# One more use of an adding DMA: the weights' low parts in the memory and attention phases of a hybrid encoder

## The reference

```python
for i in range(DEPTH):                                   # 2 layers
    h = rmsnorm(x, pre_g[i]); mem_n = rmsnorm(mem, mem_g[i])
    # layer 0: Mamba-2 SSD mixer; layer 1: neighbourhood attention, 32 heads
    proj = h @ w_in                                      # z, mixer inputs, q_mem
    kv = (mem_n @ w_mem_kv)                              # keys and values of 256 memory tokens
    m = softmax(q_mem k^T / 16) v                        # 4 memory heads of 256
    mixed = concat([mixer(proj), m]) * silu(z)           # (layer 0 norms the mixer part)
    x = x + rmsnorm(mixed @ w_out[i], post_g[i])
```

## Time and profile before

| | |
|---|---|
| time, median of 3 runs | 2127.89 us (2126.92 to 2128.80) |
| profiled execution, its own time | 2128.9 us |
| its span | 2127.1 us |
| TensorE busy | 2083.0 us (98%) |
| TensorE weight loads (beside the matmuls) | 1774.5 us (83%) |
| VectorE / ScalarE / GpSimd busy | 1074.4 / 799.7 / 883.1 us |
| bytes moved by DMA | 211.96 MB, mean 100 GB/s |
| adding DMAs, issued by GpSimd | 53, of 512 KB each |
| stores of `macc_dram` and `x1_dram` | 3072 KB each |
| a load of decay rows (`acs_dram`, line 1291), 16 times | 1536 KB each |
| residual and partial-sum loads in layer 1's memory phase | 512 KB each |
| residual loads at the end (line 2145) | 1536 and 1024 KB |

### The profile page before, as it was taken

How to read it: one execution, slowest core, us unless ns; L and a number is a source line. 1 busy time by engine, 2 the same in 40 slices (tenths; PEclk the granted TensorE clock), 3 DMA queues, 4 the chain that set the end, 5 groups by cost and what they waited for, 6 DMA issues and landing times.

```text
span 2127.1 us, 30983 instructions
## 1 busy us (share of the span) xinstructions
PE 2083.0 (98%) x12412; PEld 1774.5 (83%) x12412; DVE 1074.4 (51%) x1880; ACT 799.7 (38%) x1943; POOL 883.1 (42%) x676
## 2 busy tenths in 40 slices
PE   8999999999999999999999999999999999999997
PEld 7888887788888888877888887888888888888885
DVE  4104332598898889887602223154333414542446
ACT  4123122465564656653322211143324323432353
POOL 5533332232333332225733332664454445544543
PEclk9999999999999999999999999999999999999998
DMA  5221112466666566566421111322131223122213
GB/s 188 90 71 53 51 50 77 151 153 150 149 154 150 146 154 164 139 163 195 159 68 50 51 50 57 113 65 69 52 96 59 59 61 95 57 60 81 67 51 119
DMA packets 214316, 211.96 MB, mean 100 GB/s; under 512 B 24764, under 2 KB 173532, under 8 KB 214173
## 3 DMA queue, kind: packets, MB, share of 16 engines
q1 hardware_dynamic: 206541, 182.20, 28.3%
q0 software_dynamic: 7632, 27.79, 6.9%
HBM read 168.19 MB, written 12.21 MB: 85 GB/s over the span
## 4 chain that ended last, share of the span: by engine, by line
PE 51%; DVE 3%; issue 1%; ACT 0%; DMA 0%; POOL 0%; DVEq 0%; POOLq 0%
PE bank L246 25%; PE bank L301 9%; PE bank L647 6%; PE bank L2485 2%; PE bank L2513 2%; PE bank L1140 2%; PE bank L2496 2%; PE bank L1166 1%; DVE acc L1013 1%; PE bank L1204 1%; DVE acc L1017 1%; PE bank L520 0%; DVE acc L1007 0%; DMA R<-macc_dram 0%; PE bank L2557 0%
## 5 line engine op out<-in xcount | busy, mean ns | idle before, releaser
L246 PE MATMUL bank<-Hh,Wh 128*128 128x512 f32 (+1 forms) x1936 | 652.8, 343 | 4.8 <-ACT R L1342 1.5
L246 PE MATMUL bank<-Hl,Wh 128*128 128x512 f32 (+1 forms) x1936 | 640.6, 337 | 0.0
L246 PE MATMUL bank<-Hh,Wl 128*128 128x512 f32 (+1 forms) x1936 | 566.4, 336 | 1.2 <-DMA Wl<-Wraw 1.1
L190 POOL TENSOR_SCALAR Wh<-Wraw 128x1024 fp32r<-128x1024 f32 x164 | 176.3, 1075 | 742.2 <-issue 555.9
L246 PEld LDWEIGHTS bank<-Hh,Wh 128*128 128x128 f32 x1936 | 367.0, 190 | 52.9 <-issue 12.7
L193 POOL TENSOR_TENSOR Wl<-Wraw,Wh 128x1024 fp32r<-128x1024 f32 x164 | 404.8, 2468 | 13.7
L246 PEld LDWEIGHTS bank<-Hl,Wh 128*128 128x128 f32 x1936 | 367.3, 190 | 37.0 <-issue 1.7
L246 PEld LDWEIGHTS bank<-Hh,Wl 128*128 128x128 f32 x1936 | 348.3, 190 | 40.0 <-DMA Wl<-Wraw 1.6
L371 DVE TENSOR_TENSOR acc<-bank,acc 128x512 f32<-128x512 f32 x240 | 164.0, 690 | 163.3 <-PE bank L301 150.4
L216 POOL TENSOR_SCALAR Wl<-Wraw 128x1024 fp32r<-128x1024 f32 x53 | 68.4, 1291 | 371.8 <-DMA Wraw<-in_ssd_w_in_dram 107.9
L301 PE MATMUL bank<-Wh,Mh 128*128 128x512 f32 x384 | 151.8, 395 | 6.4 <-DVE acc L371 6.4
(11 more groups left out here) (269 smaller groups left out, 3495.2 us busy)
## 6 DMA issues: line engine op xcount, KB each, us to landing
Wraw<-in_na_w_in_dram SPq DMA_DIRECT2D x80, 512.0 KB, 3.7
Wraw<-in_ssd_w_in_dram SPq DMA_DIRECT2D x57, 512.0 KB, 4.0
Wl<-Wraw POOLq DMA_DIRECT2D x53, 512.0 KB, 4.8
Wraw<-in_w_out_dram SPq DMA_DIRECT2D x48, 512.0 KB, 3.3
R<-acs_dram SPq DMA_DIRECT2D x16, 1536.0 KB, 7.5
Wraw<-in_w_mem_kv_dram SPq DMA_DIRECT2D x32, 512.0 KB, 3.9
R<-gs_dram SPq DMA_DIRECT2D x32, 128.0 KB, 3.5
R<-R SPq DMA_DIRECT2D x32, 128.0 KB, 3.4
```

The costliest lines, as they stand in the source:

```text
L190: pool.tensor_scalar(Wh[:, s, :], Wraw[:, s, :], 1.0, 1.0, ALU.mult, ALU.mult).then_inc(pool_c, 1)
L246: mm = pe.matmul(DB[h.k % 2][:, 0:t1 - t0], w[:, k, :], x[:, k, t0:t1], start=(i == 0), stop=(i == 3 * KC - 1))
```

## The change

All units from the third on are made by the adding transfer, in every phase: `split_unit` hands over to `split_unit_by_dma` when `low_count` is positive. Units 0 and 1 (the first two key units, which are multiplied together) stay as they were. In `pe_dense` and `pe_out_tiles` the order with low products last was there already and now applies everywhere. The two loops that have their own code get the same order: in `ValueBlock.tensor` and in the value units of `memory_phase`, all tiles do their four high products first, then, behind one `wait_low`, all tiles do the two low ones. In `out_by_tile` the wait is put ahead of the tile; in `keys_by_group` it does nothing, as units 0 and 1 are not counted.

```diff
         def split_unit(pool):
             u, c = U["pool"], CH["pool"]
+            if low_count(u.k):
+                split_unit_by_dma(pool)
+                return
             s = u.k % 2
...
-        BY_DMA = {}
+        FIRST_BY_DMA = 2
 
         def low_count(unit):
-            first, last = BY_DMA["units"]
-            return unit - first + 1 if first <= unit < last else 0
+            return max(0, unit - FIRST_BY_DMA + 1)
...
                         for k in range(2):
-                            for p, (x, y) in enumerate(((Hh, wh), (Hl, wh), (Hh, wl))):
-                                mm = pe.matmul(self.banks[t][:, :], x[:, 2 * j + k, tok], y[:, k, :],
-                                               start=(j == 0 and k == 0 and p == 0), stop=(j == 3 and k == 1 and p == 2))
+                            for p, x in enumerate((Hh, Hl)):
+                                pe.matmul(self.banks[t][:, :], x[:, 2 * j + k, tok], wh[:, k, :],
+                                          start=(j == 0 and k == 0 and p == 0), stop=False)
+                    wait_low(pe, u.k)
+                    for t in range(NT):
+                        tok = slice(self.tokens[t], self.tokens[t] + P)
+                        for k in range(2):
+                            mm = pe.matmul(self.banks[t][:, :], Hh[:, 2 * j + k, tok], wl[:, k, :],
+                                           start=False, stop=(j == 3 and k == 1))
                         if t == NT - 1:
                             mm.then_inc(unit_done, 1)
                         elif j == 3:
...
                             if g == 0:
                                 pe.wait_ge(w_ready, w.value + u + 3)
+                                wait_low(pe, w.k + u)
...
                         for k in range(2):
-                            for p, (x, y) in enumerate(((Mem_h, wh), (Mem_l, wh), (Mem_h, wl))):
-                                mm = pe.matmul(V_BANK[t][:, :], x[:, 2 * j + k, tok], y[:, k, :],
-                                               start=(j == 0 and k == 0 and p == 0), stop=(j == 3 and k == 1 and p == 2))
+                            for p, x in enumerate((Mem_h, Mem_l)):
+                                pe.matmul(V_BANK[t][:, :], x[:, 2 * j + k, tok], wh[:, k, :],
+                                          start=(j == 0 and k == 0 and p == 0), stop=False)
+                    wait_low(pe, w.k)
+                    for i, t in enumerate(V_ORDER[half]):
+                        tok = slice(t * P, (t + 1) * P)
+                        for k in range(2):
+                            mm = pe.matmul(V_BANK[t][:, :], Mem_h[:, 2 * j + k, tok], wl[:, k, :],
+                                           start=False, stop=(j == 3 and k == 1))
...
             unit0, half0, mix0 = pre.units - 4, pre.half - 8, MX["pe"].k + 4
-            BY_DMA["units"] = pre.units, pre.units + unit_index(PAIRS) - 4 + 2
...
                         pe.wait_ge(w_ready, u.value + (3 if at < 2 else 4))
+                        wait_low(pe, u.k + (0 if at < 2 else 1))
```

## The result

Four runs of the changed kernel gave a median of 2187.66 us (2183.62 to 2192.79), four of the kernel before beside them 2128.35 us (2126.92 to 2130.43). The ratio is 1.0278 (95% interval 1.0262 to 1.0294): 59.3 us slower. I had predicted 2152.5 us, 2135 to 2166. The sign was right, the size less than half of what came.

What follows compares the result with a forecast made beforehand. TensorE, busy 2083.0 of 2127.1 us, was taken to bound the kernel. Terms 4 + 9 + 7 + 0.7 (attention's first key unit) + 5.5 - 1.5 = +24.7 us gave 2153.6, stated as 2152.5 us, range 2135 to 2166.

Steps and rivals of the forecast that it cites:

- What bounds: Whole kernel: TensorE is busy 2083.0 of 2127.1 us; what counts is whether GpSimd's work per unit fits TensorE's unit time.
- Term 1: First layer, value units: GpSimd's period of 6.2 us against 5.7 us per unit on TensorE, +4 us (+1 to +6.5).
- Units of 768 columns or six output tiles (8 us and more on TensorE) leave it hidden: Longer units, including most of attention: they cover the chain negate, add, land, negate, so attention costs and gains nothing there.
- Term 2: Second layer, key units: quiet chain +2.4 us, more from adds behind other loads and sync's queue; +9 us (+2.4 to +13).
- Term 3: Second layer, last two value units: an add lands late behind the `x1_dram` store and the clock falls; +7 us (+4 to +9).
- Term 4: The end, last output unit: whole landing counts, residual loads in flight, clock falls; +5.5 us (+2.4 to +7.5).
- Term 6: Order of the products: the same matmuls, so nothing; perhaps 0.3 us at the change of half, inside other stalls.
- term 5: Gain: GpSimd computes less per unit, shortening TensorE's wait for VectorE shortly before 2076 us; -1.5 us (-3.8 to 0).
- E: Rival, worse: second layer's keys saturate DMA, late residuals hold up VectorE and the turning; beyond +35, near 2170 us; chance 0.15.
- A: Rival: landing about 4.0 us in quiet stages keeps the chain hidden, only the end costs; 2128 to 2131 us; chance 0.06.
- B: Rival: faster through VectorE, its wait before 2076 us and waits for plain splits gone; 2121.8 us; chance 0.04.
- C: Rival: slower at quiet prices, the chain binds but transfers hardly meet; +9.8 us, near 2138 us; chance 0.22.

Runs made afterwards that it cites:

- experiment 5: Changed kernel with one landing semaphore for each slot of `Wl`, so GpSimd's next negation need not wait for the last add: 2173.31 us (1.0211).
- experiment 7: Changed kernel, but the transfer copies `Wraw` over `Wl` instead of adding it (low parts wrong): 2149.04 us (1.0095).
- experiment 4: Kernel before in its splits (only the mixer's units by adding transfer), but with the value units' changed loops, low products last: 2130.04 us (1.0003).
- experiment 6: Changed kernel, but the two loads of `ssd_d` read contiguous rows of 16 numbers instead of single 4-byte pieces: 2173.14 us (1.0204).
- Experiment 8: Changed kernel, but twelve loads of partial sums and residual in the second layer's memory phase move 32 of 1024 columns: 2173.14 us (1.0205).
- experiment 9: Changed kernel with both 32-column loads of partial sums and residual and one landing semaphore for each slot of `Wl`: 2171.09 us (1.0188).
- `attn_plain`: Changed kernel, but the 76 units of the attention phase are split by GpSimd alone: 2178.62 us (1.0235).

## Why the prediction was right in sign and too small

**What bounds** was right: only TensorE's idle time counts, and the loss is where units last 5.6 to 5.7 us on TensorE. The chain negate, add, land, negate became the bound there (experiments 5 and 7), attention hides it (window 1430 to 2110), and the order costs nothing (experiment 4).

**Term 1 was mis-sized, 8 us against 4.** I took the period from one pair of negations in the mixer, 6.2 us. It is 6.39 us over the eight links beside the value units. The unit time was too long as well: my 45.6 us end with a wait of 0.69 us for ScalarE, and a value unit takes TensorE 5.6 us (67.31 to 106.50, seven units). Eight links of 6.39 - 5.6 = 0.8 us make 6.3 us, of 6.7 measured; 1.3 us more had been lost in the key units (the delay goes from 0.6 to 1.9 us before the first value unit), whose loss I had not counted in this layer. One pair of rows was too thin, since with a period so near to the unit time 0.3 us in their difference raise the loss by more than half; my upper bound was +6.5.

**The step that failed outright: "Units of 768 columns or six output tiles (8 us and more on TensorE) leave it hidden".** It compares the quiet period with the unit and never asks which transfers stand ahead of an add at each place. In the first layer's heads these are the small constants of the mixer. In the kernel before they were harmless, since TensorE never waited there (no wait in its rows from 113 to 175 us). An add lands 21.2 us after its issue, and 8 us of cover do not help. It cost +14 us (experiment 6), and the trace of before had the two loads; its line 1308 (now 1323) alone, issued at 119.7 and 120.5:

```profile
DMA to landing us min/median/max: 12.6/17.2/21.8
```

It even had what they do to a transfer behind them. The weight load of 512 KB that sync issued next, and its landing (line 169 alone):

```profile
125.37 0.40 SPq L169 DMA_DIRECT2D Wraw<-in_ssd_w_in_dram  x1
```
```profile
DMA to landing us min/median/max: 18.6/18.6/18.6
```

The four weight loads before it took 3.7 to 4.1 us. I had walked sync's queue for the stages that I costed, not for those that I had called covered.

**Term 2 was mis-sized, 21.0 us against 9 (bound 13).** I started the chain at the second key unit ("the first negation can start at 974.73"). The first one, whose split came 11 us earlier in before, is the worst: its add meets five loads at once. By my own rate, 5.5 us for 1536 KB, 2560 KB would have made 9 us; 5.9 us over quiet were measured. Against 4.7 us quiet, the seven landings (10.6, 9.1, 7.1, 5.1, 5.7, 6.1, 6.2) hold 17.0 us of contention, and two stretched negations 1.8 us; I had counted four or five of 1.8 us. Together with quiet links (7 x 6.45 = 45.2) that is 64.0 us for the measured 63.3. Experiment 8 confirms the split: 13 us go with the loads. I had named sync as a second path for 1.5 us. With the chain's wait gone the key units still lose 12.1 us (experiment 5), and with thin loads 5.6 us (experiment 9), and in both traces every weight load there is issued just after an add has landed. How much sync's wait costs by itself, with the chain in place, was not measured: no run takes that wait away.

**Terms 3, 4 and 6 were right, term 5 in part by luck.** The add beside the `x1_dram` store landed after 10.0 us (11.3 at its twin), TensorE waited 4.0 us for it, and the place lost 7.9 us (+7). The end lost 6.7 us (+5.5), 2.6 of them clock. At VectorE's wait 2.0 us are won (-1.5): the wait fell from 2.1 to 1.6 us, and the clock no longer dropped behind it. The change's own part is the 0.5 us. The wait is 1.3 to 1.7 us in all eleven traces with attention's low parts by transfer and 2.1 to 2.2 us in the three without (before, experiment 4, `attn_plain`); but `attn_plain`, with a wait of 2.19 us, shows a clock of 1.00 behind it. So the 1.5 us of clock can come back without the change, and that the shorter wait is what brought them here is not shown. Attention's first units lost 1.4 us (+0.7), a small term that came out double.

**The rivals.** E, "worse", came closest in time (2170 against 2187.7), and its mechanism is that of the key units (that late residual tiles hold up VectorE was not tested). A and B failed as argued: the add is never under 4.5 us. C's transfers that "hardly meet" failed at the key units. Missing among them was a transfer held up by something other than bytes.

## What to carry to other kernels

When work moves from an engine to a DMA, list for every stage, the covered ones too, what stands in the DMA queues in the microseconds before each new transfer: its landing there is the price, not its quiet duration. A buffer hand-over that waits for a landing puts the whole landing into the period of its units, so convert only units whose time on the bounding engine is well above that period; 34 of 162 converted units made all the loss here, and one of them, with 8 us of cover, more than any other. A result that many units use with slack and a few without it should be priced on the few, each at its own place.

## What the runs showed of the hardware that I had not expected

- A transfer within SBUF that adds takes 4.5 to 4.7 us for 512 KB, the same one as a copy 2.9 us (experiment 7): accumulating costs 1.6 us or more.
- Two loads of 1024 pieces of 4 bytes, 8 KB in all, took up to 21.8 us and delayed a 512 KB transfer from another queue to 21.2 us (19.7 as a copy), while for most of that time the DMA engines' share was 0.05 and no bytes moved. As contiguous rows they took 2.6 us (experiment 6). Weight loads behind them in their own queue took 18.6 us (before) and 21.9 us (after), in place of about 4. A low DMA share was no sign that a transfer would be quick.
- GpSimd's negation took 1.81 and 2.11 us, in place of 1.05, where it ran beside VectorE's combination of three SBUF tensors:

```profile
998.15 3.27 DVE L1015 SCALAR_TENSOR_TENSOR acc<-acc,rssd,R 128x1024 f32<-128x1024 f32 x2
...
1009.90 1.28 DVE L1015 SCALAR_TENSOR_TENSOR acc<-acc,rssd,R 128x1024 f32<-128x1024 f32 x1 [2.52 <-DMA R<-macc_dram]
```

In both cases VectorE had started first. The Trainium skill, SBUF — State Buffer (SBUF: two separate sides), says that a VectorE instruction with two SBUF inputs and a GpSimd instruction that reads SBUF exclude each other, and that the one that starts first keeps the shared ports to its end. The numbers agree (2.11 us is 1.05 plus most of the 1.28 us); no run here took VectorE's instruction away.
